# The opening of a three-block transformer kernel: who sends c and the tokens, and where low parts, scaling and the small weights stand

## The reference

```python
c_act = jax.nn.silu(c)
for i in range(DEPTH):
    mod = c_act @ mod_w[i] + mod_b[i]              # 1024 x 9216 weights per layer
    sh1, sc1, g1, sh2, sc2, g2, sh3, sc3, g3 = jnp.split(mod, 9, axis=-1)
    h = modulate(rmsnorm(x, norm_g[i, 0]), sh1, sc1)
    x = x + 0.5 * g1[:, None, :] * swiglu(h, ffn_w13[i, 0], ffn_w2[i, 0])
    ...
```

## Time and profile before

| | us |
|---|---|
| median of three runs | 1746.79 |
| lowest, highest | 1744.55, 1747.05 |
| the profiled execution | 1747.42 |
| its span in the profile | 1745.3 |
| first product of the feed-forward part starts | 47.47 |

### The profile page before, as it was taken

One profiled execution on the slowest core, in us unless ns is written; L12 is line 12 of the kernel. 1 busy time (PEld: TensorE's weight loads), 2 busy tenths in 40 slices (PEclk: granted clock), 3 DMA queues, 4 the chain that ended last, 5 costly groups with the idle time before them and its releaser, 6 DMA issues.

```text
span 1745.3 us, 31824 instructions
## 1 busy us (share of the span) xinstructions
PE 1660.1 (95%) x11260; PEld 1496.9 (86%) x11260; DVE 1284.6 (74%) x2125; ACT 931.8 (53%) x1665; POOL 94.5 (5%) x164
## 2 busy tenths in 40 slices
PE   5999999999999999999989999999989899999998
PEld 5899989988899889999877888889987789988886
DVE  6888888668888888876556666669969666456665
ACT  1444457645444444445566655563648775455553
POOL 2000010300000100000001000010000000000000
PEclk9999999999999999999999999999999999999999
DMA  9888867857888878876524656644454246445651
GB/s 347 298 294 301 305 181 192 171 193 259 295 302 296 269 272 292 298 244 193 176 87 144 212 180 204 192 151 151 153 160 134 83 158 193 134 151 190 195 185 62
DMA packets 129432, 361.94 MB, mean 207 GB/s; under 512 B 10058, under 2 KB 58714, under 8 KB 119488
## 3 DMA queue, kind: packets, MB, share of 16 engines
q1 hardware_dynamic: 111200, 262.18, 46.8%
q10 hardware_dynamic: 12432, 78.65, 13.9%
q0 software_dynamic: 5712, 19.92, 3.5%
HBM read 353.47 MB, written 7.23 MB: 207 GB/s over the span
## 4 chain that ended last, share of the span: by engine, by line
PE 65%; DVE 17%; issue 7%; ACT 6%; DMA 2%; POOL 1%; ACTq 1%; DVEq 0%; POOLq 0%
PE ps L883 45%; PE ps L1224 9%; PE ps L1225 4%; DVE w_lo L232 4%; DVE arena L387 3%; DVE arena L2877 2%; ACT w_hi L226 2%; DMA resid<-in_x 1%; ACT w_hi L1282 1%; DVE resid L1501 1%; DVE w_lo L1293 1%; PE ps L744 1%; DVE act_s L1370 1%; DMA gate_scratch<-gcol 1%; ACTq L361 1%
## 5 line engine op out<-in xcount | busy, mean ns | idle before, releaser
L883 PE MATMUL ps<-t_both,w_hi 128*128 128x256 f32 x3852 | 709.8, 286 | 9.1 <-DVE arena L2851 4.4
L883 PEld LDWEIGHTS ps<-t_both,w_hi 128*128 128x128 f32 x3852 | 600.5, 191 | 21.5 <-issue 9.4
L883 PE MATMUL ps<-t_both,w_lo 128*128 128x256 f32 x1926 | 545.1, 283 | 0.0
L1293 DVE TENSOR_TENSOR w_lo<-raw,w_hi 128x1024 fp32r<-128x1024 f32 x258 | 313.7, 1222 | 82.6 <-ACT w_hi L1282 82.4
L232 DVE TENSOR_TENSOR w_lo<-raw,w_hi 128x1024 fp32r<-128x1024 f32 x240 | 288.6, 1224 | 114.1 <-ACT w_hi L226 113.8
L883 PEld LDWEIGHTS ps<-t_both,w_lo 128*128 128x128 f32 x1926 | 367.7, 191 | 0.2
L1282 ACT ACTIVATE w_hi<-raw 128x1024 fp32r<-128x1024 f32 x258 | 268.9, 1053 | 119.1 <-PE ps L883 79.2
L226 ACT ACTIVATE w_hi<-raw 128x1024 fp32r<-128x1024 f32 x240 | 247.3, 1052 | 136.9 <-PE ps L883 97.5
L1224 PE MATMUL ps<-t_both,w_hi 128*128 128x512 f32 x640 | 226.7, 398 | 0.0
L883 PE MATMUL ps<-w_hi,g_hi 128*128 128x512 f32 x440 | 177.3, 403 | 13.7 <-DVE g_lo L1373 11.6
L1225 PE MATMUL ps<-t_both,w_lo 128*128 128x256 f32 x640 | 179.7, 281 | 0.0
(11 more groups left out here) (397 smaller groups left out, 1764.3 us busy)
## 6 DMA issues: line engine op xcount, KB each, us to landing
raw<-in_stream SPq DMA_DIRECT2D x498, 512.0 KB, 4.6
arena<-in_mod_w ACTq DMA_DIRECT2D x72, 1024.0 KB, 7.2
grow<-gate_scratch POOLq DMA_DIRECT2D x6, 512.0 KB, 7.3
u_scratch<-u_keep ACTq DMA_DIRECT2D x1, 3072.0 KB, 36.9
arena_for_products<-mem_scratch POOLq DMA_DIRECT2D x3, 1024.0 KB, 6.3
mem_scratch<-arena_for_products POOLq DMA_DIRECT2D x1, 2048.0 KB, 12.1
arena<-u_scratch POOLq DMA_DIRECT2D x8, 256.0 KB, 3.3
small<-in_small POOLq DMA_DIRECT2D x1, 1368.0 KB, 10.9
```

The costliest lines, as they stand in the source:

```text
L883: last = TE.matmul(out, lhs, rhs, start=start and i == 0, stop=stop and i == 2)
L1293: VE.tensor_tensor(w_lo[:, s, :], raw[:, s, :], w_hi[:, s, :].bitcast(F32), ALU.subtract).then_inc(lo_done, 1)
```

## The change

It makes five edits in the opening. (1) The eight columns of c come by a transfer of their own at the head of ACT's queue, with a semaphore of their own, and silu(c) waits for that alone; the other columns stay on GpSimd's queue. (2) The tokens go from GpSimd's queue to SP's, behind blocks 0 and 1. (3) The small weights wait for the second half of chunk 3 in place of the second half of chunk 1. (4) VectorE makes the low part of block 0 between the halves of chunk 0 and that of block 1 behind it, then chunks 1 and 2, then scales the tokens, and then makes chunk 3. (5) The eight matmuls that keep TensorE busy ahead of the turn of chunk 2 go.

```diff
+        c_in = sem("c_landed")
...
             for s in range(RING):
                 if s == 2:
+                    sp.dma_start(x[:, :, :], a["x"].rearrange("(q p) d -> p q d", p=P)).then_inc(x_in.sem, x_in.up(16))
                     sp.wait_ge(mod_landed[0][1], 32)
                 sp.dma_start(raw[:, s, :], a["stream"][s, :, :]).then_inc(landed[s], 16)
...
-            for dst, src in ((cols[:, :], a["cols"]), (cst[:, :], a["const"])):
+            for dst, src in ((cols[:, 8:], a["cols"][:, 8:]), (cst[:, :], a["const"])):
                 pool.dma_start(dst, src).then_inc(first_in.sem, first_in.up(16))
...
-            pool.dma_start(x[:, :, :], a["x"].rearrange("(q p) d -> p q d", p=P)).then_inc(x_in.sem, x_in.up(16))
...
-            pool.wait_ge(mod_landed[1][1], 16)
+            pool.wait_ge(mod_landed[0][1], 32)
             pool.dma_start(small[:, :], a["small"]).then_inc(small_in.sem, small_in.up(16))
...
+            act.dma_start(cols[:, 0:8], a["cols"][:, 0:8]).then_inc(c_in, 16)
             for c in range(3):
                 for half in range(2):
                     mod_load(act, half, c)
-            act.wait_ge(first_in.sem, first_in.n)
+            act.wait_ge(c_in, 16)
             E.activation(cact[:, :], col("c", 0, 8), ACT.Silu).then_inc(A.sem, A.up())
...
                 if scale_after:
-                    dve.wait_ge(first_in.sem, first_in.n)
                     dve.wait_ge(A.sem, silu_at)
-                    for c in range(scale_after):
+                    for half in range(2):
+                        mod_products(dve, 0, range(4 * half, 4 * half + 4), first=True)
+                        split_lo(dve, half)
+                    for c in range(1, scale_after):
                         mod_products(dve, c, range(KT), first=True)
-                    for h in range(blocks["hi"]):
-                        split_lo(dve, h)
...
-        normalize(lambda q: x[:, q, :], lambda q: ar(XN, QT, D)[:, q, :], first_norm, landed_first=x_in, scale_after=2)
+        normalize(lambda q: x[:, q, :], lambda q: ar(XN, QT, D)[:, q, :], first_norm, landed_first=x_in, scale_after=3)
...
-            for c in range(2, PRE):
+            dve.wait_ge(first_in.sem, first_in.n)
+            for c in range(3, PRE):
                 mod_products(dve, c, range(KT), first=True)
             split_lo(dve, 2)
...
             mod_turn(pe, 1, first=True)
-            keep_busy(ps[4], 8)
             mod_turn(pe, 2, first=True)
```

## The result

The changed kernel took 1751.76 us (median of 14 runs, 1749.08 to 1752.93), the kernel before 1745.59 in the same measurement (14 runs, 1744.12 to 1747.34): ratio 1.0032, 95% interval 1.0025 to 1.0039. It is 5.6 us slower by the ratio. The forecast was 1749.4, within a range of 1746.6 to 1752.6, with a chance of 0.32 for more than 3.5 us slower. The profiled execution took 1751.75, its span 1749.8.

A forecast was written before the change was run, and what follows sets the result against it. The prediction took the opening to hang on VectorE's chunk 3, feeding TensorE's last turn. GpSimd's held operations +1.6 and TensorE's clock +1.0 gave +2.6 on the median 1746.79, so 1749.4 us, range 1746.6 to 1752.6.

The forecast's parts named there:

- The likeliest case: Opening: GpSimd's late operations cost +1.6 and TensorE's lower clock +1.0, together +2.6, giving 1749.4 us; chance 0.45.
- the slower rival: GpSimd behind the small weights' wait: held longer, +3.9 + 1.0 = +4.9, 1751.7, up to 1753; chance 0.30.
- the hold: GpSimd's token-sum operations, behind the small weights' wait for chunk 3, delay VectorE's scaling: chunk 3 ends at 43.4, +1.6 us.
- The start: VectorE's opening: with c's own transfer it starts near 8.7 in place of 13.63; alone it would end at 38.6 to 40.6.
- The tokens: Tokens on SP's queue: may land 1 us earlier or 2 later than 23.17; nobody waits, so 0.
- The clock: TensorE's opening without eight fillers: last turn at 1.2 GHz, +0.84, transposes +0.15, together +1.0.
- both kernels are alike: TensorE after the opening's turn and transposes: first product starts at 1.2 GHz in either kernel, so 0.
- I carry the shift to the end: From TensorE's first product to the end: the opening's shift stays unchanged, as the same work follows in the same order.
- a difference that first appears behind 60 us: Sign that the forecast is wrong: the two kernels' traces first differ after the opening, behind 60 us.

The follow-up runs named there:

- the powers first: Changed kernel with GpSimd's wait for chunk 3 and issue of the small weights moved behind its four operations on the token sums: 1746.94 us, ratio 1.0010.
- the early fillers: Changed kernel with eight fillers added ahead of the bias tables, where TensorE waits anyway: 1748.47 us, ratio 1.0016 to the kernel before.
- the kernel before with the small weights late: Kernel before with one edit alone, the small weights waiting for chunk 3 in place of chunk 1: 1754.29 us, ratio 1.0051.
- four and four: Changed kernel, small weights issued behind GpSimd's four operations, four fillers ahead of the bias tables, ten (not six) ahead of the last turn: 1743.86 us, ratio 0.9991.

## Why the prediction was right or wrong

The time was in the range, and the sign was right. The likeliest case, +2.6, did not come: measured beside its own kernel before, the change costs 5.6. The range was met in part by luck. The kernel before came out 1.2 us under the 1746.79 that the sum starts from, and the slower rival's 1751.7 is the measured time to 0.1 us for a reason that was not its own: its hold was +3.9, the hold was +1.0, and the stall stood in no rival.

- **The hold** was right in place and mechanism. Chunk 3's issue of the small weights came at 32.63 (32.8 forecast), the powers followed at once, the wait at L520 was 2.05 + 0.71. Its size at the end of chunk 3 was +1.0 in place of +1.6: GpSimd's operations took 0.30, 0.57, 0.86 and 0.55, shorter than the rows that I took. Their sum is 2.28, against 2.66 in the forecast and 3.97 in the earlier trace rows; the other 0.2 is the earlier landing. The 0.86 lay beside VectorE's scaling and ended with it, the other three while VectorE stood idle. With the powers first, beside VectorE's products, they took 0.68, 0.96, 0.42 and 1.02, or 3.08. The Trainium skill (GPSIMD Engine Reference, Specifications) says that GpSimd and VectorE share their way into SBUF and hinder each other where a VectorE instruction has two inputs there; by that rule they are short because VectorE stands idle, and the sums agree, the 0.42 does not.
- **The start** at 8.7 was 10.6: the first half of chunk 0, issued at 1.19, needed 9.3 us in place of 7.5. It didn't matter, and VectorE without the hold ended at 39.8, in the 38.6 to 40.6 forecast.
- **The tokens** priced at 0 were mis-sized. Nobody waits for them, that was right, but edit 2 decides when the chunks land: the same VectorE order without it ends 2 us later.
- **The clock** was right for the profiled executions (1.91 in the last turn), at +0.84 for the turn. What I had at 0, "both kernels are alike" after it, was wrong: in its second profile the kernel before goes on at 2.4 GHz through its first products, and that is worth 1.9 us more. The profile that I had was the unlucky kind, 1.8 above the median of the fourteen later runs; I saw 0.6 over the median of three and took it for noise.
- **The step that failed** is "From the first product on, the same work follows in the same order, nothing is tied to an absolute time, so I carry the shift to the end." The order of work was the same, but the place of TensorE's instructions in its program was not. Edit 5 has a price of 2.4 us, or 3.9 where the clock falls behind it, some 300 us later, which no view of the opening could show and no rival named. The prediction's own sign of being wrong, "a difference that first appears behind 60 us", is what came.

By the runs, the 5.6 us are: 4.4 for edit 5, which go when the fillers come back, and 1.2 for the rest, where the profile has 1.0 for the hold at the end of chunk 3. Of the 4.4, the early fillers take back 2.8, the stall with what follows it; the 1.6 left would be the clock in the opening. Edit 5 is shown twice, by the fillers put back and by the kernel before without them (4.9). The hold is shown by the powers first and by the kernel before with the small weights late. The 1.6 for the clock is argued: the intervals of the two kernels with fillers overlap. What sets the clock in one execution and not in another is open, and so is why one program length needs a late fetch, or whether it is the length or the place of the instructions: no kernel with another number of fillers was tried.

## What to carry to other kernels

Before a wait is moved later, read what the same engine has to do behind it, even if that engine is hardly used; put the issue behind those operations instead. Take instructions out of a busy engine's program only with the whole trace compared, matmul by matmul: here one jump of the shift, 300 us behind the edit, came with a fetch of instructions. And before the first profile is taken for the typical one, look where its time lies among the runs.

## What the hardware did unexpectedly

- A TensorE program shorter by 32 instructions stands 2.2 to 2.3 us near 334 us, in five of five profiles, with a 16 KB fetch starting with the stall; at the full length it starts some 17 us ahead of the place, and there is no stall, in nine of nine. Eight fillers more took it away in each of the three places tried (ahead of the turn of chunk 2, ahead of the bias tables, four and four). Behind the stall the granted clock fell to half in two of the five (from 336.2 to 339.6 and from 333.4 to 336.8), which cost 1.5 us more.
- The granted clock in the opening is not a property of the kernel. With the same program it rose at 37.7 or 38.4 and fell at 44.5 or not before 82.8. In the changed kernel with the fillers back and no gap over 0.1 us in TensorE's work from 16.4 to 46.2 us it rose only at 50.3; with the same TensorE program and the powers first it rose at 39.0.
- With the same 1 MB of tokens issued on GpSimd's queue at 4.1 us rather than on SP's at 1.7, VectorE waits for chunk 2 and ends chunk 3 2.0 us later (41.8 against 39.8).
